# Feed-forwards of a streaming encoder trunk: the Strassen form from the third gate/up pair on, three weight sums on GpSimd, activation sums ahead of weight blocks

## The reference

```python
def swiglu(h, w1, w2):
    g, u = jnp.split(h @ w1, 2, axis=-1)
    return (jax.nn.silu(g) * u) @ w2
...
        hn = modulate(rmsnorm(x, norm_g[l, 0]), sh1, sc1)
        x = x + 0.5 * g1[:, None, :] * swiglu(hn, ffn_w1[l, 0], ffn_w2[l, 0])
...
        x = x + g2[:, None, :] * m
        hn = modulate(rmsnorm(x, norm_g[l, 2]), sh3, sc3)
        x = x + 0.5 * g3[:, None, :] * swiglu(hn, ffn_w1[l, 1], ffn_w2[l, 1])
```

## Time and profile before

| | us |
|---|---|
| median of 3 runs | 1444.4 (1443.32 to 1444.68) |
| the profiled execution's own time | 1445.51 |
| its span | 1443.9 |
| TensorE busy | 1422.3 |
| VectorE busy | 1014.5 |
| ScalarE busy | 663.6 |
| GpSimd busy | 71.5 |

### The profile page before, as it was taken

The page is one execution under the profiler, slowest core; times in us unless marked ns, Lnnn a source line. Parts: engine busy times, 40 slices in busy tenths (PEclk is TensorE's granted clock), DMA queues, the critical chain, the costliest instruction groups (busy, mean ns, idle before and its releaser), DMA issues.

```text
span 1443.9 us, 25671 instructions
## 1 busy us (share of the span) xinstructions
PE 1422.3 (99%) x10202; PEld 1372.2 (95%) x10202; DVE 1014.5 (70%) x1742; ACT 663.6 (46%) x1186; POOL 71.5 (5%) x121
## 2 busy tenths in 40 slices
PE   7999999999999999999999999999999999999998
PEld 6899999999999999999789999998999999999997
DVE  5767677676776776667886567557767676767776
ACT  5543525253435444666825453226425253444354
POOL 3100000000000130000100000004000000000001
PEclk9999999999999999999999999999999999999999
DMA  9752434444344612231362222444324233231222
GB/s 319 213 187 61 159 105 146 117 147 147 110 139 132 184 30 74 74 93 54 98 187 77 67 73 63 133 143 122 110 56 143 67 88 88 71 105 52 81 74 74
DMA packets 219564, 161.02 MB, mean 112 GB/s; under 512 B 6858, under 2 KB 204678, under 8 KB 219458
## 3 DMA queue, kind: packets, MB, share of 16 engines
q1 hardware_dynamic: 217490, 153.89, 35.7%
q0 software_dynamic: 1696, 5.56, 1.3%
q10 hardware_dynamic: 272, 0.10, 0.0%
HBM read 151.50 MB, written 8.03 MB: 110 GB/s over the span
## 4 chain that ended last, share of the span: by engine, by line
PE 92%; DVE 3%; DMA 2%; ACT 1%; POOL 1%; issue 1%; SPq 0%; DVEq 0%; ACTq 0%; POOLq 0%
PE acc L864 25%; PE acc L1196 19%; PE pC L1087 18%; PE acc L1087 14%; PE acc L1075 4%; PE pB L986 2%; PE acc L1145 2%; PE pC L1336 1%; DMA ada_raw<-in_w_ada 1%; DMA raw<-in_ffn_w 1%; PE pB L945 1%; PE pB L1321 1%; PE pC L1471 1%; PE pC L1355 1%; PE acc L881 0%
## 5 line engine op out<-in xcount | busy, mean ns | idle before, releaser
L1569 ACT ACTIVATE slot<-raw 128x512 fp32r<-128x512 f32 (+1 forms) x310 | 189.7, 616 | 239.4 <-PE acc L1196 137.8
L2142 DVE TENSOR_TENSOR slot<-raw,slot 128x512 fp32r<-128x512 f32 (+1 forms) x310 | 208.6, 677 | 53.8 <-ACT slot L1569 51.3
L1196 PE MATMUL acc<-hid_hi,slot 128*128 128x320 f32 x1240 | 238.5, 310 | 0.0
L1087 PE MATMUL pC<-hn_hi,slot 128*128 128x320 f32 x912 | 216.3, 309 | 0.0
L1196 PEld LDWEIGHTS acc<-hid_hi,slot 128*128 128x128 f32 x1240 | 195.1, 188 | 2.9 <-issue 2.1
L864 PE MATMUL acc<-hn_hi,whi 128*128 128x320 f32 x672 | 161.5, 322 | 0.0
L1087 PEld LDWEIGHTS pC<-hn_hi,slot 128*128 128x128 f32 x912 | 156.2, 188 | 2.5 <-issue 2.5
L864 PE MATMUL acc<-hn_hi,wlo 128*128 128x320 f32 x672 | 153.5, 310 | 0.0
L864 PE MATMUL acc<-hn_lo,whi 128*128 128x320 f32 x672 | 153.5, 310 | 0.0
L1087 PE MATMUL acc<-tT,slot 128*128 128x320 f32 x912 | 146.3, 309 | 0.0
L1196 PE MATMUL acc<-hid_lo,slot 128*128 128x320 f32 x620 | 142.0, 308 | 0.0
(11 more groups left out here) (389 smaller groups left out, 2404.3 us busy)
## 6 DMA issues: line engine op xcount, KB each, us to landing
raw<-in_ffn_w SPq DMA_DIRECT2D x86, 512.0 KB, 5.1
sraw<-in_w_ada SPq DMA_DIRECT2D x26, 1024.0 KB, 7.2
wraw<-in_w_in SPq DMA_DIRECT2D x36, 512.0 KB, 3.6
raw<-in_ffn_w SPq DMA_DIRECT2D x16, 1024.0 KB, 5.0
ada_raw<-in_w_ada SPq DMA_DIRECT2D x8, 1024.0 KB, 11.0
wraw<-in_w_out SPq DMA_DIRECT2D x16, 512.0 KB, 4.2
raw<-in_ffn_w SPq DMA_DIRECT2D x8, 768.0 KB, 4.4
sraw<-in_w_ada_final SPq DMA_DIRECT2D x6, 1024.0 KB, 7.5
```

The lines of the kernel that those rows point to most:

```text
L1087: last = mm(out, w[:, kk * P:(kk + 1) * P], a, start=(first and kk == 0 and t == 0), stop=(kk == KQ - 1 and t == 2), skip_group_check=not ...
L1196: last = mm(a[h], w[t // 2][:, k, :], (hid_hi, hid_lo)[t % 2][:, k * TOK + h * HALF:k * TOK + (h + 1) * HALF], start=(k == 0 and t == 0), ...
L1569: A(slot_as(fi, b, 0), source_of(fi, b), ACT.Copy).then_inc(blk_hi, 1)
L2142: V.tensor_tensor(out=slot_as(fi, b, 1), in0=source_of(fi, b), in1=slot_as(fi, b, 0).bitcast(F32), op=ALU.subtract).then_inc(blk_lo, 1)
```

## The change

`PLAIN` goes from 3 to 2, so pair 2 of each feed-forward takes the Strassen form: 12 matmuls fewer, 3 blocks more, 4 weight sums more and the t sums needed one pair earlier. Three of the four weight sums of that first Strassen pair are given to GpSimd (`weight_sums`), behind its share of the norm. On VectorE the t sums all go into pair 0, ahead of blocks 7, 8 and 9 of the weights, and on ScalarE `t_high` likewise; `hid_low` of pair 0 comes later. The slots are handed out in another rotation; each block still follows the block seven before it.

```diff
-PLAIN = 3
+PLAIN = 2
...
-    SLOT0, RAW0 = (2, 4), (0, 1)
+    SLOT_OF, RAW0 = ((0, 1, 2, 3, 6, 4, 5), (4, 5, 6, 0, 1, 2, 3)), (0, 1)
...
+        def weight_sums(fi):
+
+            r, n = JOB_PAIR[PLAIN], wino_before(fi, PLAIN)
+            w = raw[raw_of(fi, r)]
+            a11, a21, a22 = w[:, 0:WB], w[:, 2 * WB:3 * WB], w[:, 3 * WB:4 * WB]
+            if fi:
+                pool.wait_ge(unit_done, U_END)
+            else:
+                pool.wait_ge(ch_tr, ADA_FIRST)
+            pool.wait_ge(raw_in[raw_of(fi, r)], raw_count(fi, r))
+            s_sum_first(s1w[:, :], a21, a22, ALU.add)
+            pool.wait_ge(s_sum, 4 * n + 1)
+            s_sum_first(a21, a11, a21, ALU.subtract)
+            s_sum_first(s2w[:, :], s1w[:, :], a11, ALU.subtract)
...
         norm_samples(0, None, 0, KD)
+        weight_sums(0)
...
         norm_samples(3, None, 6 * KD, 7 * KD)
+        weight_sums(1)
...
         def plain_pair(fi, p):
 
             b = BLK_PAIR[p]
-            if p == 1:
-                t_high(fi, 1)
             act.wait_ge(blk_done, fi * NB + b + 2)
             A(split2(silg[:, :]), halves(acc[0]), ACT.Silu).then_inc(silu_done, 1)
             if p == 0:
                 t_high(fi, 0)
-            if p == 1:
-                t_high(fi, 2)
-            if p == 2:
-                t_high(fi, 3)
+                t_high(fi, 1)
             blk(fi, b + 7)
-            blk(fi, b + 8)
+            if p:
+                blk(fi, b + 8)
             act.wait_ge(blk_done, fi * NB + b + 4)
-            if p == PLAIN - 1:
+            if p:
                 t1_high(fi)
             hid_high(fi, p)
+            if p == 0:
+                t_high(fi, 2)
+                blk(fi, b + 8)
+                t_high(fi, 3)
             blk(fi, b + 9)
             blk(fi, b + 10)
...
         def t_sums(fi, kk):
 
             a, b, n = hn_f(kk), hn_f(kk + KQ), 3 * (KQ * fi + kk)
+            if kk >= 2:
+                dve.wait_ge(t_ready, 6 * fi + kk - 1)
...
             b = BLK_PAIR[p]
             if p == 0:
                 t_sums(fi, 0)
-            if p == 1:
                 t_sums(fi, 1)
-                t_low(fi, 1)
-                t_sums(fi, 2)
-            if p == 2:
-                t_sums(fi, 3)
-                t_low(fi, 3)
+            else:
                 blk(fi, b + 7)
                 blk(fi, b + 8)
             dve.wait_ge(blk_done, fi * NB + b + 4)
...
-            if p < PLAIN - 1:
-                t_low(fi, (0, 2)[p])
+            if p == 0:
+                t_low(fi, 0)
+                t_sums(fi, 2)
+                t_low(fi, 1)
                 blk(fi, b + 7)
+                t_sums(fi, 3)
+                hid_low(fi, p)
+                t_low(fi, 2)
                 blk(fi, b + 8)
+                t_low(fi, 3)
             else:
                 t1_low(fi)
-            hid_low(fi, p)
+                hid_low(fi, p)
             blk(fi, b + 9)
             blk(fi, b + 10)
```

More of the change, by code:

```diff
@@ L458, in slot_of @@
     def slot_of(fi, b, lo, cols):
-        return slots[(b + SLOT0[fi]) % SLOTS][:, lo * WB:lo * WB + cols]
+        return slots[SLOT_OF[fi][b % SLOTS]][:, lo * WB:lo * WB + cols]
     def source_of(fi, b):
@@ L800, in norm_samples, with s_sum_first @@
                 nc.gpsimd.tensor_tensor(out=to, in0=tv, in1=per_stream[1], op=ALU.add).then_inc(tms_ready, 1)
+        def s_sum_first(out, in0, in1, op):
+            nc.gpsimd.tensor_tensor(out=out, in0=in0, in1=in1, op=op).then_inc(s_sum, 1)
+        def weight_sums(fi):
[11 more added lines that the diff above has]
+            s_sum_first(s2w[:, :], s1w[:, :], a11, ALU.subtract)
         norm_samples(0, None, 0, KD)
+        weight_sums(0)
         pool.wait_ge(blk_done, BLK_DOWN[-1])
@@ L2107, in first_sums @@
         def first_sums(fi, b):
-            if b not in BLOCK or BLOCK[b][0] != "wino" or BLOCK[b][2] or (fi, b) in summed:
+            if b not in BLOCK or BLOCK[b][0] != "wino" or BLOCK[b][2] or BLOCK[b][1] == PLAIN or (fi, b) in summed:
                 return
@@ L2131, in blk @@
                 first_sums(fi, b)
-                if j == 1:
+                if j == 1 and p > PLAIN:
                     if n:
```

## The result

| | before | with the change |
|---|---|---|
| median, us | 1444.51 (1443.09 to 1445.41, 6 runs) | 1453.24 (1450.47 to 1454.76, 6 runs) |
| ratio | | 1.0061 (1.0050 to 1.0071) |
| profiled execution, us | 1445.51 | 1453.15 |
| its span, us | 1443.9 | 1451.5 |
| its granted clock | 0.998 | 0.994 |

The kernel became 8.7 us slower; 4.9 us were forecast, and the time lies 0.2 us above the range. The page, part 1, answers to the earlier trace rows: TensorE has 24 matmuls less in the program (98% busy), VectorE and GpSimd are busy longer.

A forecast was written before the change was run, and what follows sets the result against it. TensorE, busy 99% of the span, was taken to bound the kernel. Waits of 0.8 + 3.0 and 1.8 + 2.8 us, 8.4 together, less 3.5 gained gave +4.9 and 1449.3 us; range 1444.2 to 1453.0 for 8 in 10.

The forecast's parts named there:

- 12 matmuls fewer in each feed-forward, 1.76 us: TensorE, pair 2: a Strassen pair has 84 matmuls instead of 96, saving 1.76 us per feed-forward, 3.5 us for both.
- VectorE's chain of 17.2 us, `hidp` of pair 1 at 67.3: VectorE, feed-forward 0: gapless work from 50.02 puts product `hidp` of pair 1 at 67.3, without GpSimd's delays.
- From `hidp` to TensorE's third product 3.35 us, and 3.0 in feed-forward 1: Through ScalarE's queue to snapshot `s0` of pair 2: 3.35 us in feed-forward 0 with `duo_row`, 3.0 in feed-forward 1.
- A sum on GpSimd costs VectorE 1.0 us, three in each feed-forward: Before `hidp` of pair 1: turns with GpSimd delay VectorE 3.0 us in feed-forward 0, 2.8 in feed-forward 1.
- Waits of 3.8 and 4.6 us: TensorE waiting for `s0` in pair 2: 0.8 + 3.0 us in feed-forward 0, 1.8 + 2.8 in feed-forward 1.
- the wait for block 7: TensorE may wait for block 7's low part; not added, since the later wait for `s0` takes it in.
- The sum, 1449.3: Whole kernel: waits of 8.4 us less 3.5 gained make +4.9 us, predicted time 1449.3 us.
- the clock: Rival: TensorE's clock drops after the gap, costing 7 us over two products in each feed-forward, time 1456; chance 0.09.
- In pair 2 VectorE works off what it is behind: Pair 2: VectorE needs some 9.3 us against TensorE's 12.3, so nothing was added for later waits.
- The range: Whole kernel: 1444.2 to 1453.0 us for 8 in 10; the forecast's own range 1446.5 to 1452.5.
- the sums are nearly hidden: Rival: a GpSimd sum costs VectorE 0.21 us or less, time 1444.7 down to 1443.5; chance 0.15.
- the change is faster: Rival: snapshot `s0` is never late in pair 2, time 1440.9; chance 0.08.

The follow-up runs named there:

- the last kernel: The change with weight sums on VectorE, snapshots first on ScalarE in pairs 2 and 3, `hidp` of pair 1 ahead of blocks 11 and 12: 1443.21 us, ratio 0.9989.
- the sums cut short: The changed kernel with GpSimd's three sums cut to 8 of 512 columns, so its output is not the reference's: 1443.55 us, ratio 0.9999.
- the kept-busy run: The changed kernel with 9 matmuls of 128x256 where TensorE would wait for snapshot `s0` of pair 2, feed-forward 1 only: 1450.86 us, ratio 1.0046.
- the snapshots first: The changed kernel, GpSimd's sums kept, with ScalarE's first pair 2 snapshots ahead of `hid_high` and the last two blocks of pair 1: 1446.43 us, ratio 1.0020.
- the kernel with both faults mended: The changed kernel with the three weight sums on VectorE and ScalarE's pair 2 snapshots ahead of `hid_high` of pair 1: 1446.06 us, ratio 1.0010.

## Why the prediction was wrong, step by step

- *12 matmuls fewer in each feed-forward, 1.76 us.* Nothing contradicts it; the page has 24 matmuls less, and the last kernel shows part of it as time.
- *VectorE's chain of 17.2 us, `hidp` of pair 1 at 67.3.* Right: 67.31 with the sums cut short.
- *From `hidp` to TensorE's third product 3.35 us, and 3.0 in feed-forward 1.* Right: 70.46 to 73.73, 3.27, and 1026.71 to 1029.71, 3.0.
- *A sum on GpSimd costs VectorE 1.0 us, three in each feed-forward.* Right: 1.0 to 1.1 each by the rows, and `hidp` 3.15 us later than with short sums (70.46 against 67.31); 2.8 in feed-forward 1, as forecast. The scaling by columns from sums of 128 to sums of 512 that it rested on held: 4 x 0.27 = 1.1, and 1.15 by the rows. As to the rule of the Trainium skill (SBUF — State Buffer, Who interferes with whom): the trace agrees, since each held-up VectorE instruction ends only 0.35 us after a GpSimd sum, and each sum ends 1.15 us after a VectorE instruction, so that with its own wait it is listed with 1.42 to 1.76 us.
- *Waits of 3.8 and 4.6 us.* Right: 2.2 + 1.8 = 4.0 in feed-forward 0 by the shift of what follows, and 4.7. They are losses in sum and not single waits: one wait of 1.8 us and what TensorE was late by before it, and 3.8 us with 0.8 for `hn_lo`. That the wait for block 7 wasn't to be added was right as well.
- *The sum, 1449.3.* Here the prediction failed: it took the rival "the clock" as an alternative with a chance of 0.09 and left it out of the time. It isn't an alternative: it follows from the wait that the forecast itself had. The step that failed is the clock term, put at nothing in the sum: from "no row shows what it does after such a gap" a small chance was made, where a gap of 4 us inside dense work needed a term. No row of before has such a gap, so only its bounds could be worked out, 0 and 7 us, and the sum took the lower one. It measured 2.6 us in the profile and 2.4 by the kept-busy run, in feed-forward 1; the price written down, 1.76 for each product of 12 matmuls at the lower level, was somewhat high (1.5 and 1.1 more for the two products). In feed-forward 0 the gap is 1.8 us, and the products behind it run at their usual length in the change's profile; behind the same gap the kernel with 9 matmuls lost 1.5 us. With this term the sum is 1451.8. What is left, 1.4 us, is mostly the 1.1 between profiled execution and median: the change's profiled execution lies on its median and the earlier one above its own, so the sum against the medians came out 1 us low. The range's upper end, 1453.0, reached "somewhat into the clock's case" without a term worked out for it; that the result lies only 0.2 us above it is luck.
- *In pair 2 VectorE works off what it is behind.* Right for the changed kernel, but only because TensorE stands still: with the snapshots first TensorE waits for VectorE at the start of pair 3 (1.11, 1.42, 0.77 us).
- *The range.* Its lower end for the forecast, 1446.5, is given for "0.2 to 0.5 us a sum", but belongs to 0.5 alone; 0.2 gives 1444.7 by the same terms.
- *The rivals.* That the sums are nearly hidden, and that the change is faster, are out.

How often the clock falls after a given gap stays open, and why it falls at 42 and at 618 us, where TensorE waited under 1 us or not at all. One run of six of the changed kernel took 1450.47 with a granted clock of 0.997 where the others have 0.994 or 0.995; that would be the run in which it did not fall, but no profile of it was taken. The median of the kernel with both faults mended (1446.06) is also above what its profiled execution shows (1444.92), and this wasn't followed up: seven of its eleven runs lie at 1445.7 to 1446.5 us, six of them with a granted clock of 0.997, and four at 1444.2 to 1445.1 with 0.998 or 0.999. A slow stretch more, of some 1.5 us, would fit; no profile of such a run was taken.

## What to carry to other kernels

When an engine is made late, ask which queue passes the lateness on: here ScalarE's snapshot, ready to be taken, stood behind a copy that waited for VectorE, and turning the two round gave back 6.8 of 8.7 us (5.9 by ratios). Work given to GpSimd is not free where VectorE is busy with two-input instructions on SBUF; a 512-column sum cost VectorE 1.0 us there and 0.6 us if it made the sum itself. And a stall of TensorE that is forecast should be priced with the clock behind it.

## What was unexpected of the hardware

A wait of 3.83 us inside dense work brought the granted clock to 0.50 in the 5 us behind it and cost 2.6 us on top of itself; 9 otherwise useless float32 matmuls in the gap took 2.4 us off the time. In two profiled executions the clock fell after a wait of 1.8 us (products of 3.21 in place of 1.92 us and of 3.32 in place of 2.03), while waits of 1.8, 2.0 and 2.2 us in others passed without a fall. And VectorE and GpSimd, both with work queued, took turns one instruction at a time, 1.15 us for a sum of 512 columns.
